# An expert's down matrix loaded as neighbouring rows, with the hidden columns in that order from a strided moving operand

## The reference, cut to what matters

```python
# 32 experts, each w_gate and w_up (1024 x 512), w_down (512 x 1024); 512 slots (token, expert), sorted by expert
xs = t[tok]
hid = jax.nn.silu(lax.ragged_dot(xs, w_gate, sizes)) * lax.ragged_dot(xs, w_up, sizes)
out = lax.ragged_dot(hid.astype(xs.dtype), w_down, sizes)
out = out * weights[order][:, None].astype(out.dtype)
y = jnp.zeros_like(t).at[tok].add(out.astype(t.dtype))
```

## Time and profile before

| | us |
|---|---|
| median of 3 runs | 1663.4 (1659.41 to 1666.94) |
| the profiled execution | 1666.0 |
| its span, first to last instruction | 1663.9 |
| mean granted clock of TensorE | 0.931 |

### The profile page before, as it was taken

One profiled execution on the slowest core, in us unless ns is written; L12 is line 12 of the kernel. 1 busy time (PEld: TensorE's weight loads), 2 busy tenths in 40 slices (PEclk: granted clock), 3 DMA queues, 4 the chain that ended last, 5 costly groups with the idle time before them and its releaser, 6 DMA issues.

```text
span 1663.9 us, 19274 instructions
## 1 busy us (share of the span) xinstructions
PE 1388.6 (83%) x7296; PEld 1003.2 (60%) x7297; DVE 530.2 (32%) x854; ACT 363.1 (22%) x530; POOL 52.6 (3%) x75
## 2 busy tenths in 40 slices
PE   4968999979888889998797889858877777777766
PEld 3857999968545689998675677743322222222224
DVE  2355545446655165453303344240000000000002
ACT  2153433310034143332200452111000000000001
POOL 1000000001012000000000000000000000000000
PEclk9989999999976899999899999959999999999987
DMA  8416455349900255650865122223999999999961
GB/s 301 152 51 202 152 195 184 101 156 360 374 19 1 76 181 174 202 176 26 307 250 208 51 101 102 83 78 116 421 421 422 424 421 422 425 421 421 425 252 74
DMA packets 118787, 371.46 MB, mean 223 GB/s; under 512 B 4801, under 2 KB 52274, under 8 KB 110546
## 3 DMA queue, kind: packets, MB, share of 16 engines
q1 hardware_dynamic: 111536, 344.28, 54.1%
q0 software_dynamic: 6832, 26.39, 4.4%
q10 hardware_dynamic: 370, 0.11, 0.0%
HBM read 361.31 MB, written 9.44 MB: 223 GB/s over the span
## 4 chain that ended last, share of the span: by engine, by line
PE 51%; DMA 28%; DVE 10%; ACT 6%; issue 2%; SPq 1%; ACTq 0%; POOL 0%; POOLq 0%; DVEq 0%
DMA ys<-big 22%; PE ps L1348 16%; PE ps L1295 11%; PE ps L1279 8%; DMA wbuf<-in_w_ada 3%; PE ps L1495 3%; PE ps L1286 3%; PE ps L1599 2%; DVE big L988 2%; PE ps L1258 2%; DMA wbuf<-in_w_up 1%; SPq L458 1%; ACT big L808 1%; PE ps L1635 1%; PE ps L1577 1%
## 5 line engine op out<-in xcount | busy, mean ns | idle before, releaser
L1599 PE MATMUL ps<-wbuf,big 128*64 128x512 f32 x1024 | 244.5, 632 | 52.6 <-DMA wbuf<-in_w_up 48.5
L1348 PE MATMUL ps<-big_parts,parts 128*128 128x256 f32 x2112 | 261.6, 286 | 8.6 <-DVE big_parts L915 8.5
L1348 PEld LDWEIGHTS ps<-big_parts,parts 128*128 128x128 f32 x2112 | 259.0, 194 | 10.0 <-issue 9.3
L1599 PEld LDWEIGHTS ps<-wbuf,big 128*64 128x64 f32 x1024 | 85.3, 145 | 210.2 <-issue 189.3
L1279 PE MATMUL ps<-big,wbuf 128*128 128x256 f32 x896 | 200.4, 386 | 10.6 <-DVE big L845 6.7
L915 DVE TENSOR_TENSOR parts<-wbuf,parts 128x2048 fp32r<-128x2048 f32 x66 | 150.9, 2292 | 172.5 <-ACT parts L631 108.2
L1279 PEld LDWEIGHTS ps<-big,wbuf 128*128 128x128 f32 x896 | 172.4, 193 | 36.0 <-issue 8.5
L1235 DVE TENSOR_TENSOR big<-big,ps 128x256 f32<-128x256 f32 x32 | 13.5, 421 | 437.7 <-ACT big L805 437.7
L1295 PE MATMUL ps<-big_parts,parts 128*128 128x256 f32 x1056 | 134.0, 288 | 8.8 <-DVE parts L915 8.8
L1613 PE MATMUL ps<-wbuf,big 128*64 128x512 f32 x512 | 122.0, 618 | 19.5 <-DVE big L1237 19.5
L1295 PEld LDWEIGHTS ps<-big_parts,parts 128*128 128x128 f32 x1056 | 131.8, 197 | 9.2 <-DVE parts L915 9.2
(11 more groups left out here) (245 smaller groups left out, 1069.3 us busy)
## 6 DMA issues: line engine op xcount, KB each, us to landing
wbuf<-in_w_gate SPq DMA_DIRECT2D x32, 2048.0 KB, 18.0
wbuf<-in_w_up SPq DMA_DIRECT2D x32, 2048.0 KB, 22.4
wbuf<-in_w_down SPq DMA_DIRECT2D x32, 2048.0 KB, 27.0
wbuf<-in_ffn_w_in SPq DMA_DIRECT2D x44, 1024.0 KB, 7.9
wbuf<-in_w_ada POOLq DMA_DIRECT2D x12, 2048.0 KB, 11.4
wbuf<-in_ffn_w_out SPq DMA_DIRECT2D x22, 1024.0 KB, 5.1
wbuf<-in_w_in SPq DMA_DIRECT2D x10, 2048.0 KB, 7.9
wbuf<-in_attn_w_qkv SPq DMA_DIRECT2D x6, 2048.0 KB, 14.2
```

Of the source, the lines that this page charges most:

```text
L1348: ins = mm(ps[:, b, d * 256:(d + 1) * 256], w[pw][:, k, d * P:(d + 1) * P], h_part_of[px][:, k], start=(k == 0 and i == 0), stop=(k == KC ...
L1599: ins = mm(at, x[:, k], gu_place[s][:, :, k, h * 256:(h + 1) * 256], start=(k == 0), stop=(k == KC - 1))
```

## The change

w_down is read with `(p k)`, k = 4: partition p holds rows 4 p to 4 p + 3, which lie next to each other in HBM (16 KB). The hidden columns must follow: chunk i of the hidden product must hold columns i, 4 + i, 8 + i and so on. So the gate/up matmul's moving operand is now a view with three free dimensions: matrix m, j (two of the four column classes for each half h) and f (128 columns, 4 apart). Half h computes the classes 2 h and 2 h + 1, and PSUM is written in the same places, in runs as before. The transposes, `hidT` and the down matmuls are untouched in code; chunk i now multiplies rows 4 p + i of w_down. `EC` is 4.

```diff
         def load_down(eng, s, e):
-            eng.dma_start(d_place[s], a["w_down_2"][0, bass.ds(e, 1)].rearrange("e (k p) f -> p (e k) f", p=P)).then_inc(d_loaded[s], 16)
+            eng.dma_start(d_place[s], a["w_down_2"][0, bass.ds(e, 1)].rearrange("e (p k) f -> p (e k) f", k=EC)).then_inc(d_loaded[s], 16)
...
                 for k in range(KC):
                     for h in range(2):
-                        at = ps[h * WIN:(h + 1) * WIN, 0, :].rearrange("p (m f) -> p m f", m=2)
-                        ins = mm(at, x[:, k], gu_place[s][:, :, k, h * 256:(h + 1) * 256], start=(k == 0), stop=(k == KC - 1))
+                        at = ps[h * WIN:(h + 1) * WIN, 0, :].rearrange("p (m j f) -> p m j f", m=2, j=2)
+                        w = gu_place[s][:, :, k].rearrange("p m (f j) -> p m j f", j=EC)[:, :, 2 * h:2 * h + 2]
+                        ins = mm(at, x[:, k], w, start=(k == 0), stop=(k == KC - 1))
                 ins.then_inc(gu_done[q], 1)
```

## The result

| | us |
|---|---|
| before, median of 4 runs | 1662.95 (1659.41 to 1666.94) |
| after, median of 4 runs | 1838.36 (1832.71 to 1846.27) |
| ratio, with 95% interval | 1.1057 (1.1005 to 1.111) |
| span of the execution profiled, before and after | 1663.9 and 1830.7 |

The kernel became slower by about 175 us. The prediction said slower by 139 us, 1802, with a range from 1654 to 1838.

What follows compares the result with a forecast made beforehand. The DMA was taken to bound the expert loop at 15.49 us; the strided read makes TensorE the bound at 12.50 + 6.88 = 19.38 us an expert, +138.9 us over 32, giving 1802 us, range 1654 to 1838.

Steps and rivals of the forecast that it cites:

- TensorE's reserve of 2.99 us: Expert loop: TensorE needs 12.50 us an expert against the DMA's 15.49, leaving 2.99 us spare.
- the row of the weight loads: Gather products' stationary loads at stride 8: 313 ns against 190 contiguous at full clock, 335 against 333 at half clock.
- part 1: Down load in 16 KB runs: saves 0.23 us a load, 6.4 us in all, only while the DMA is the bound.
- part 2: Gate/up's moving operand read every fourth fp32 value: taken at half-clock pace, 13.76 us an expert, 6.88 more.
- The upper end: Gate/up's strided read priced from durations: 0.96 ns more a column, 7.87 us more an expert.
- The sum: Expert loop with TensorE as bound: 12.50 + 6.88 = 19.38 us an expert, 620.2 us for 32, +138.9 us.
- a fall of the clock: Rival: clock falls while the array is fed at half pace; down takes 7.3 us, about 1919 us; chance 0.03.
- the upper price: Expert loop with 7.87 us more gate/up: 20.37 us an expert, +170.5 us, 1834 us.
- Hidden stride: Rival: gate/up's strided read stays below 9.87 us, DMA still sets the pace; 1657 us, 1654 to 1663; chance 0.25.
- Partial penalty: Rival: gate/up takes between 1.43 and 1.85 times today's; 1714 us at 1.6, range 1670 to 1780; chance 0.07.
- Shared limit: Rival: gate/up's two column halves share one strided limit; 27.5 us, period 33.1, some 2242 us; chance 0.03.
- The down load not doing what it says: Rival on w_down's load: covered by part 1's lower end, no gain; matters only if the stride is hidden; no chance given.

Runs made afterwards that it cites:

- pairs: Changed kernel, but gate/up's moving view reads two neighbouring fp32 values, then steps 16 bytes; transposes take every second column of the product; 1657.4 us, ratio 0.9961 to before.

## Why the prediction was right, and where it was wrong

**Right: what bounds, and what changes hands.** TensorE's reserve of 2.99 us was used up, PE took the DMA's place on the chain, and the store's landing left it. The cost came from the strided stream alone, and its pace did not depend on the clock (0.90 us a turn at 0.50 and at 1.00), as the row of the weight loads had said.

**Right: part 1.** 0.19 us a down load where 0.23 was taken, 15.30 us a period, 1660 us by itself, against 1657 forecast, and nothing of it to be seen in the changed kernel.

**Wrong: the size of the strided stream.** The step that failed is the value taken in part 2. From rows that gave a duration (313 against 190 ns, 0.96 ns more a column) I took instead the pace of the array at half its clock, because the times were alike, and so 6.88 us more an expert. Measured: 14.41 - 6.88 = 7.53 us, 0.92 ns a column. Over 32 experts the 0.65 us are 20.8 us. The upper end, 7.87, was the nearer one. Half the array's clock was never the mechanism; it is a price of 1.76 ns a line that lies close to 2 x 0.84. The durations, read to their end, would have said so: 190 ns less 128 columns at 0.83 leave 84 ns that don't depend on the columns, and (313 - 84) / 128 = 1.79 ns a column, an estimate from the earlier trace rows. That row has a stride of 8, and the moving operand with a stride of 8 took 14.70 / 8192 = 1.79 ns, 14.70 us where the upper end makes 6.88 + 7.87 = 14.75. So at its own stride the row did carry over to the other input, in this one comparison; a stride of 4 costs 2% less.

**Wrong: the clock.** The sum gave every down product 3.67 us, and a fall of the clock was a rival at 0.03 with all of them slow. What happened is its small form: 7 of 32, 11.4 us. The trace of before had the warning, slow down products and slow gate/up in its own loop, which the prediction didn't read. The two misses and 0.2 us of the first gate/up, which overlaps no down product, make 32.4 of the 32.8 us by which the loop is longer than the sum (1780.17 + 3.67 - 1130.88 = 652.96 against 620.2). Outside the loop this execution was 4.9 us shorter, 4.4 of it ahead of the loop, so its span grew by 166.8 us. The medians lie 175.4 apart because the execution profiled is the shortest of the changed kernel's four, 5.7 us below the median, while that of before lies 3.1 above its own; these 8.7 us no trace explains.

**Wrong: the range.** Its upper end was the upper price alone, 1834, and a little. It left out that the slow clock can come on top of any price, and that it may vary from execution to execution: the four runs of after span 13.6 us, the longest with a mean granted clock of 0.932 and the shortest with 0.944. That this difference lies in the loop is not shown, since one of them was profiled; the kernel before spans 7.5 us too. The median lies 0.4 us past the end.

**Rivals.** Hidden stride: out; it would have needed less than 9.87 us of gate/up. Partial penalty: that is what a stride of 3 gives (10.79 us, 1715 us). Shared limit: out. The down load not doing what it says: out, by the run of the down load alone.

## What to carry to other kernels

For a moving fp32 operand, count the 16-byte lines that it enters and compare the 1.76 ns a line measured here with 0.84 ns a value: two values a line were nearly free, one value a line cost twice. If a layout for DMA wants columns apart, look for an order of the same loops that keeps two neighbours together, and let a small transpose behind it take the stride. A row of the same access on another input of the engine was a good estimate here (14.75 us from the weight loads, 14.70 measured, at the same stride); use its durations, and not the nearest round mechanism. And when a change takes the bound from one engine to another, look in the trace of before for what that engine did slowly while it had time to spare.

## What the runs showed of the hardware

- A stream with a stride of 4 starts its matmuls 0.90 us apart at either granted clock, 0.50 and 1.00 in the stretches shown.
- The moving operand's price was 1.76 ns for each line entered at strides of 2, 3 and 4 and for pairs, and 1.79 ns at a stride of 8; the weight loads of stride 8 fit the same 1.79.
- Two streams side by side each have their own limit of lines; one strided stream is as slow as two (14.68 and 14.60 us).
- With strided feeds the granted clock fell in some of the down products that came right after (5.35 us instead of 3.65), while behind the first expert it stood at 1.00 in the strided matmuls themselves. With contiguous feeds that kept TensorE busy as long (gate/up done twice, 13.75 us) it never fell; with contiguous feeds and waits for the DMA, in the kernel before, it did.
- In a full queue a 2 MB down load lands 4.88 us behind the load ahead of it with 16 KB runs, and 5.08 us with 4 KB runs.
